# The gates' products in the second and fourth quarter of a unit instead of the first and third

## What is computed

```python
def peer_ffn(xn, w_query, sub_keys, expert_u, expert_v):
    q = (xt @ w_query).reshape(NT, PEER_HEADS, 2, D_KEY // 2)
    s = jnp.einsum('nhpd,pkd->nhpk', q, sub_keys)
    v1, i1 = lax.top_k(s[:, :, 0], PEER_TOPK)
    v2, i2 = lax.top_k(s[:, :, 1], PEER_TOPK)
    ...
    idx = e1 * N_KEYS + e2
    gate = jax.nn.softmax(best, axis=-1)
    ...
        act = jax.nn.gelu(jnp.einsum('cd,ced->ce', xc, expert_u[ic]), approximate=False)
        return jnp.einsum('ce,ced->cd', (gc * act), expert_v[ic])
```

## Time and profile before

| | |
|---|---|
| median of 3 runs | 4199.19 us (4188.9 to 4200.55) |
| the profiled execution | 4189.57 us |
| its span | 4187.8 us |
| TensorE busy | 4000.8 us, 96% |
| VectorE, GpSimd, ScalarE busy | 60%, 55%, 36% |
| mean of a split L381 on ScalarE | 1.91 us |
| mean of a remainder L398 on GpSimd | 4.64 us |
| mean of a row L1480 on VectorE | 2.28 us |
| moved by DMA | 899.46 MB, 215 GB/s over the span |

### The profile page before, as it was taken

One profiled execution on the slowest core, in us unless ns is written; L12 is line 12 of the kernel. 1 busy time (PEld: TensorE's weight loads), 2 busy tenths in 40 slices (PEclk: granted clock), 3 DMA queues, 4 the chain that ended last, 5 costly groups with the idle time before them and its releaser, 6 DMA issues.

```text
span 4187.8 us, 69486 instructions
## 1 busy us (share of the span) xinstructions
PE 4000.8 (96%) x27233; PEld 3552.2 (85%) x27233; DVE 2514.5 (60%) x3407; ACT 1502.8 (36%) x2053; POOL 2309.9 (55%) x930
## 2 busy tenths in 40 slices
PE   7999999999999999999999889999999999999997
PEld 5777777777878787789999789999989999999997
DVE  4343334444455453267774566666638888898885
ACT  4333223333322221133333766666522223323233
POOL 4333233333233444435455456676768899999784
PEclk9999999999999999999999999999999999999998
DMA  3222222222132434233334579999989999999892
GB/s 124 91 84 80 87 84 87 87 87 87 71 116 80 146 135 146 90 139 124 134 125 150 216 314 370 364 371 373 367 321 393 367 400 393 395 400 392 316 380 104
DMA packets 258400, 899.46 MB, mean 215 GB/s; under 512 B 107672, under 2 KB 140696, under 8 KB 162736
## 3 DMA queue, kind: packets, MB, share of 16 engines
q1 hardware_dynamic: 175984, 482.50, 32.1%
q0 software_dynamic: 46080, 335.56, 19.7%
q10 hardware_dynamic: 36160, 78.85, 4.9%
HBM read 828.10 MB, written 68.71 MB: 214 GB/s over the span
## 4 chain that ended last, share of the span: by engine, by line
PE 64%; issue 15%; POOL 9%; ACT 5%; DVE 3%; DMA 2%; ACTq 1%; SPq 0%; POOLq 0%; DVEq 0%
PE ps L403 14%; PE ps L405 13%; PE ps L404 13%; PE ps L1986 5%; PE ps L1988 5%; POOL wl L394 5%; PE ps L1987 5%; POOL wl L398 2%; PE ps L1676 2%; ACT stage L1047 1%; POOL rowb L672 1%; ACT wh L390 1%; ACT oh L1042 1%; POOL act L678 1%; PE ps L1935 1%
## 5 line engine op out<-in xcount | busy, mean ns | idle before, releaser
L398 POOL TENSOR_TENSOR wl<-raw,wh 128x2048 fp32r<-128x2048 f32 x268 | 1244.6, 4644 | 1656.8 <-ACT wh L381 1656.8
L403 PE MATMUL ps<-xh,wh 128*128 128x352 f32 (+1 forms) x3904 | 1437.6, 368 | 37.4 <-DVE xl L1163 18.9
L405 PE MATMUL ps<-xh,wl 128*128 128x352 f32 (+1 forms) x3904 | 1403.5, 360 | 0.0
L404 PE MATMUL ps<-xl,wh 128*128 128x352 f32 (+1 forms) x3904 | 1403.0, 359 | 0.0
L403 PEld LDWEIGHTS ps<-xh,wh 128*128 128x128 f32 x3904 | 742.6, 190 | 134.3 <-issue 44.4
L381 ACT ACTIVATE wh<-raw 128x2048 fp32r<-128x2048 f32 x270 | 516.7, 1914 | 899.6 <-PE ps L405 778.4
L405 PEld LDWEIGHTS ps<-xh,wl 128*128 128x128 f32 x3904 | 741.8, 190 | 83.6
L404 PEld LDWEIGHTS ps<-xl,wh 128*128 128x128 f32 x3904 | 742.8, 190 | 81.6 <-issue 7.7
L1986 PE MATMUL ps<-gah,wh 128*128 128x352 f32 x2048 | 666.8, 326 | 32.9 <-POOL wl L394 22.6
L1988 PE MATMUL ps<-gah,wl 128*128 128x352 f32 x2048 | 662.1, 323 | 0.0
L1987 PE MATMUL ps<-gal,wh 128*128 128x352 f32 x2048 | 660.1, 322 | 0.0
(11 more groups left out here) (335 smaller groups left out, 4257.0 us busy)
## 6 DMA issues: line engine op xcount, KB each, us to landing
raw<-stream SPq DMA_DIRECT2D x396, 1024.0 KB
gelu_scratch<-preb ACTq DMA_DIRECT2D x128, 176.0 KB
gates_scratch<-stage ACTq DMA_DIRECT2D x22, 1024.0 KB
gt<-gates_scratch SPq DMA_DIRECT2D x32, 704.0 KB
act<-gelu_scratch SPq DMA_DIRECT2D x32, 704.0 KB
mergegate_scratch<-sgb ACTq DMA_DIRECT2D x32, 256.0 KB, 2.0
sgm<-mergegate_scratch SPq DMA_DIRECT2D x32, 256.0 KB, 2.7
h_in<-x_t SPq DMA_DIRECT2D x4, 1024.0 KB, 8.7
```

The source lines that it names most:

```text
L398: pool.tensor_tensor(wl[s][:, :], raw[s][:, :], wh[s][:, :].bitcast(F32), ALU.subtract).then_inc(w_lo, 1)
L403: pe.matmul(dst, w_h, h[:, kx, lo:], start=start, stop=False)
L404: pe.matmul(dst, w_h, l[:, kx, lo:], start=False, stop=False)
L405: return pe.matmul(dst, w_l, h[:, kx, lo:], start=False, stop=stop)
```

## The change

In a unit with one block `score_parts` now cuts the unit into four parts instead of two. `between(c)` does nothing in front of parts 0 and 2; in front of part 1 it issues the block's first pair of products, in front of part 3 the second. Units with two blocks and all other engines' programs stay as they are.

```diff
             def gates_one(i, s):
-                score_parts(SC_GATES + i, s, score_unit(SC_GATES) + i, 2, lambda c: gates(GATES_TWO + i, s, c))
+                score_parts(SC_GATES + i, s, score_unit(SC_GATES) + i, 4, lambda c: gates(GATES_TWO + i, s, c // 2) if c % 2 else None)
```

## The result

The changed kernel takes 4150.69 us (median of 4 runs, 4148.42 to 4152.37); the kernel before takes 4199.87 us (4 runs, 4188.9 to 4201.99). The ratio is 0.9894, with a 95% interval of 0.9878 to 0.9911: faster by 1.1%. The span of the profiled execution fell from 4187.8 to 4146.7 us, 41.1 us.

What follows compares the result with a forecast made beforehand. TensorE was taken as the bound, losing 0.72 us in each of 64 one-block units, 46 us; DMA cut this to 40, the part behind to 38. From 4199.2 us that gave 4161, range 4142 to 4187.

Steps and rivals of the forecast that it cites:

- The cause: Units with one block: second pair waits for PSUM bank 6, as ScalarE reaches the first pair's result 2.88 us after its split.
- The unit without waits: Units with one block: 48 matmuls at 7.73 us plus two pairs at 0.24 us give 8.21 us, where 8.93 is taken.
- The covers: Slack after the move: bank 1.5 us (0.5 in store units), next split 1.4, GpSimd's remainder of the weights 1.2.
- store units: 16 of the 64 units, also storing a finished stage: ScalarE 1.0 us later, 0.5 us of cover left, TensorE's wait gone.
- The DMA term: Stretch of 64 units: 398 GB/s needed; gain 46 us at 420 GB/s or 36 at 391, so 40 taken.
- the rival of late transfers: Stores put 1 MB ahead of weights, splits come late in one unit in four: 12 to 28 us less; chance 0.20.
- a sign that would prove me wrong: In the stretch: TensorE waiting for L398, L381 waiting for raw weights, or the clock below 1.00.
- The 2 us behind the stretch: Between 3022 and 3061 us a fuller queue may lengthen waits for weights: 2 us taken off the gain.
- The base: Median of the runs before, 4199.2 us, from which 38 us were taken; the profiled execution took 4189.6.
- a DMA bound: 366 GB/s is already the most: the wait moves to the weights, time stays 4199 us, give or take 12; chance 0.10.
- Slower through the clock: Each of 16 stores makes TensorE stand 2 us and its clock fall: 59 us against 46, 13 us slower, 4212; chance 0.06.

Runs made afterwards that it cites:

- second_only: Part of the change alone, against the kernel before: first pair stays at the unit's start, second moves to the fourth quarter (slices 0 and 12); 4155.5 us, ratio 0.9905.
- first_only: The other part alone, against the kernel before: first pair moves to the second quarter, second stays at the half (slices 4 and 8); 4191.9 us, ratio 0.9997.
- act_first: Kernel before with TensorE's order kept; ScalarE empties the first pair's bank ahead of the split and the GELU of the unit before; 4160.4 us, ratio 0.9921.
- off7: Changed kernel with both pairs at the latest place, slices 7 and 15 of 16; 4150.7 us, ratio 0.99 to the kernel before.
- after_extra: Changed kernel plus a 1 MB copy from HBM to HBM in every fourth unit with one block, 16 in all; 4163.0 us.
- after: The changed kernel itself, against the kernel before; median 4150.69 us, ratio 0.9894; its profiled execution 4148.4 us.
- after_again: The changed kernel run again without edits, beside the runs with added copies; 4151.9 us, its profiled execution 4159.4 us.

## Why the prediction was right

The kernel was forecast at 4161 us (4142 to 4187), faster; it takes 4150.7.

**The cause** was right: the second pair waited for a bank that ScalarE reached late. Only second_only had the gain, first_only none, and act_first took the wait away without moving a product.

**The unit without waits** was put at 8.21 us; it takes 8.14. Pairs stand 4.07 us apart in the changed kernel, and the plain unit of 7.73 us that I added them to was a little dear. That is 0.07 x 64 = 4.5 us of gain not counted.

**The covers** held as worked out. Second conversion forecast at 6.2 us behind the split, measured 6.07, with ScalarE waiting for TensorE as said; store units lose nothing; off7 shows how much was left.

**The DMA term** came out near its size, 6 us taken: 64 x 8.14 = 521, the stretch takes 528.2, so 7.2 us went there. That is in part luck, for its course was not as I told it. I took 6 us as the middle between two rates, 391 and 420 GB/s; but after_extra moved 418, so by the rate nothing had to be lost at 398. What was lost came from single late loads, which is the mechanism of the rival of late transfers, at a lower price. I had put the splits 8.2 to 8.45 us apart, with none of 9.4 or 9.7; in 11 of the 16 units behind a store unit the next split came 9.1 to 10.0 us after the last. I also named waits of L381 for weights as a sign that would prove me wrong. They came, 25 times, with 52.3 us of idle time in front of them (a split on time has 1.44 there). Three splits in a row, and TensorE's pairs through them:

```profile
2493.92 1.91 ACT L381 ACTIVATE wh<-raw 128x2048 fp32r<-128x2048 f32 x1 [1.28 <-PE ps L405]
...
2503.68 1.91 ACT L381 ACTIVATE wh<-raw 128x2048 fp32r<-128x2048 f32 x1 [3.06 <-DMA raw<-stream]
...
2510.52 1.92 ACT L381 ACTIVATE wh<-raw 128x2048 fp32r<-128x2048 f32 x1 [0.61 <-PE ps L405]
```

```profile
2499.56 0.40 PE L1935 MATMUL ps<-oh 128*128 128x256 f32 x2
...
2503.64 0.40 PE L1935 MATMUL ps<-oh 128*128 128x256 f32 x2
...
2507.91 0.51 PE L1935 MATMUL ps<-oh 128*128 128x256 f32 x2
...
2512.38 0.40 PE L1935 MATMUL ps<-oh 128*128 128x256 f32 x2
```

The split at 2503.68 is 9.76 us behind the last, 1.6 late. The pairs behind it come 4.27 and 4.47 us apart instead of 4.07: 0.6 us lost. Three rows show where: VectorE's addition in front of the first of these two pairs, GpSimd's remainder, and the first matmul of the next unit:

```profile
2507.22 0.63 DVE L1471 TENSOR_TENSOR stage<-ps,stage 128x256 f32<-128x256 f32 x1 [2.56 <-ACT stage L1047]
```

```profile
2505.67 4.63 POOL L398 TENSOR_TENSOR wl<-raw,wh 128x2048 fp32r<-128x2048 f32 x1 [2.78 <-ACT wh L381]
```

```profile
2510.35 0.43 PE L403 MATMUL ps<-xh,wh 128*128 128x352 f32 x1
```

Half is the bank's. The late split brought the first conversion late with it, the addition ended at 2507.85, and the pair due at 2507.71 started at 2507.91 and held up the next matmul by 0.1 us more than a free pair does. The other half is the remainder's: it ended at 2510.30, and the matmul due at 2510.17 came at 2510.35. So a late load has two covers. I counted GpSimd's 1.2 us, but not that the second pair's cover in front of the bank, 1.5 us and 0.5 in a store unit, shrinks by as much as the split is late. The two covers took 1.0 of the 1.6 us, the next split came after 6.84 us, and nothing was carried on. Most of a late load was no lost time, but not all: by the starts of the splits, ten such places of 0.4 to 0.9 us each make up nearly all of the 7.2 us. The waits recorded in the stretch for either cause, 0.9 and 0.2 us, hide most of that, as they did before the change. The sign should have been both waits of TensorE, with the length of the unit beside them.

**The 2 us behind the stretch** didn't come: 1165.3 us follow it, as before. TensorE is busy for 31.3 of the first 39 us there, where it was for 32.6, but the part as a whole is no longer.

**The base** is where most of the 10 us of error lies. The sum gave 38 us against the profiled execution, and 41.1 came: 3 us. I took them off the median of three runs, 4199.2; over 63 more runs the kernel before takes 4192: 7 us. Against that median the changed kernel is 41 us faster, as its trace says. The profiled execution's own time, 4189.6, was the nearer one: 4189.6 - 38 = 4152.

**The rivals.** Late transfers came, but took 7 us and not 12 to 28; a DMA bound is out. Slower through the clock: TensorE never stood idle for 2 us in the stretch, and the clock is 1.00 there.

## What to carry to other kernels

Where one buffer goes round between engines, place the producer's step by when its consumer comes free, not evenly from the unit's start: here the engine that empties the bank was busy for the first third of each unit, and moving both writes back by 12 matmuls shortened the stretch by 43.5 us, nearly all of it through the second. Compare the length of a repeated unit with the sum of its parts (8.93 against 8.2); recorded waits (30.7 us) showed only two thirds of what was to be had. A transfer that lands late is a loss only beyond the covers behind it; look for the bound engine's own waits, all of them, since the lateness can arrive through another buffer than the one that was loaded: here 32.4 us through the bank and 0.6 through the weights.

## What was not expected of the hardware

- The 16 DMA engines of one core moved 418 to 419 GB/s over 505 us with this mix, two thirds of its packets of 8 KB or more (after_extra), and no more with more to do.
- In the units with two blocks the mean granted clock was 0.91 in the changed kernel (longest wait for the bank 3.2 us) and 0.99 in after_extra, with the same instructions there on TensorE and a longest wait for the bank of 2.6 us: 155.6 and 148.7 us.
- Executions of one kernel differ by 10 us and more (4181 to 4212 us for the kernel before), and mostly with the mean granted clock of the whole execution: a median of 4202 us at 0.982 and 4187 at 0.986. Not all of it does: after and after_again, both at 0.983, lie 11 us apart, 8.5 of them waits in the last stage.
